# Key pages of a paged attention cache: 64 page copies by SyncE against 16 row gathers by GpSimd

## The chip, the cores and the metric

The kernel runs on one core of one Trainium2 chip. The metric is the device time of one execution in microseconds. Engines go by the names of the profile: PE is TensorE, DVE is VectorE, ACT is ScalarE, POOL is GpSimd and SP is SyncE; SPq and ACTq rows are the DMA issues of SP and ACT.

## The reference, cut to what matters

One inference step of one decoder layer: 256 prompt tokens and 8 decoding sequences of 4 new tokens, D_MODEL 1024. The layer has a gated DeltaNet head group, a stick-breaking attention head group and a mixture of 32 experts (top 4). The change touches the attention of the decoding sequences over their cached past. Each of the 8 sequences has 1024 past keys and values in 8 pages of 128 rows, and a page table says which of 80 pages of the pool hold them.

```python
k_past = cache_k[0, page_table]            # (8 sequences, 8 pages, 128 rows, 8 heads, 64)
z = q . k / sqrt(64) + b_h                 # scores of 4 query tokens, 8 heads, over 1024 keys
beta = sigmoid(z)
A[t, s] = beta[t, s] * prod_{s < j < t} (1 - beta[t, j])
o = A @ v_past
```

The product runs over the keys in their order, so a sequence's scores have to stand in order of position when they are scanned. A row of the cache (8 heads of 64 float32) is 2 KB, a page is 256 KB, a sequence's keys are 2 MB and so are its values.

## The kernel before, in words

The program has a mixer part (projections, attention of the decoding sequences, causal convolution; the first 193 us), a second part (prompt attention and DeltaNet, to about 320 us), and the experts. All three live in blocks in which each engine has its own program, tied by counting semaphores.

**The ring.** All large loads of the mixer go into a ring of 12 slots of 1 MB, used as 6 pairs of 2 MB. `PAIRS` lists what is loaded in order: `w` q, `w` k, K0, K1, `w` v, K2, K3, V0, V1, `w` c0, K4, K5, V2, `w` c1, V3, K6, `w` c2, K7, V4, V5, `w` z, V6, V7 and the two halves of w_out (K and V are the keys and values of a sequence, `w` the input projection's columns for one group). Pair q may be loaded only when pair q-6 has been used (`used`): a weight group when its last projection tile is done (`s_pj`), keys when their scores are done (`s_sc`), values when they are summed (`s_av`). SP issues all of it from one queue in exactly that order (`load_pair`), with small loads after K0, the store of the new keys after K5 and of the new values after V3.

**Keys.** K of a sequence is 8 DMAs of 256 KB, each from a page whose number SP reads into a register (`value_load` from `pt`). Page pg goes to the 32 partitions 32*(pg//2) and up, and of each page the row q*32+r lands in partition r at column block q. So one DMA writes 32 partitions in runs of 2 KB. DVE then turns the tile in place in 32x32 blocks (`turn_keys`, L812, two instructions of 128x2048 a sequence), which puts 32 dimensions on the partitions and 32 rows along the columns. V of a sequence is 8 DMAs of 256 KB over all 128 partitions, in runs of 2 KB.

**PE's order.** PE goes through 29 projection tiles (`tiles`: q 0 to 3, k 4 to 7, v 8 to 11, ba 12, convolution 13 to 24, z 25 to 28), each 8 products over 288 tokens (L509, 16 matmul records a tile). The attention is put between the tiles by hand: `scores(b)` for two sequences after tiles 6, 11, 16, 22 (`SC`, L443), `turn_A(b)` after 10, 15, 19, 25, `values(b)` after 14, 19, 24, 26 (`AV`), `own_heads(b)` after 16, 21, 26, 27, and `spread_new` (L429) after tile 9, which needs the weights of the new tokens (`weights_new`, DVE L835 to L842).

**DVE's order.** DVE turns K0 and K1 before the tiles, K2 after tile 5, K3 after 8, K4 after 12, K5 after 14, K6 after 19, K7 after 20, and does the convolution (`conv`), the scans and the copies in the same queue. The new tokens' work (`mask_new`, `weights_new`) and `scan(0)` stand after tile 7, behind the turning of K2.

**POOL** builds masks and constants (L685 to L763), clears the query blocks (L725), waits at L745 for the small loads, and from tile 13 on multiplies the convolution's outcome with its sigmoid (`silu`, L766 to L772) and squares it (L782). `conv(j)` and the sigmoid of j wait for `silu(j-2)`.

**The start.** ACT issues three DMAs (norm weight, the convolution's state, its taps) and then normalises x; DVE makes the rows (L792, L793), PE turns the taps and the rows (L370, L379) and starts tile 0.

## Time and profile before

| | |
|---|---|
| time of three runs | 1267.64, 1264.80, 1265.74 us, median 1265.74 |
| span of the profiled execution, first to last instruction | 1263.3 us (no other time of it is recorded; 2.4 us under the median) |
| granted TensorE clock, mean | 0.990 of full |
| PE busy over the span | 1208.9 us (96%) |
| DVE, ACT, POOL busy | 445.0, 228.8, 87.5 us |
| bytes moved | 464.23 MB, 367 GB/s over the span |
| mixer part | 0 to 193.7 us |

The profile is one execution. Busy times are read as shares of an engine's time; PE's busy time includes matmuls that run at half clock. A wait names the engine or DMA that came last. The timeline rows give the start and length of consecutive instructions of one line, with the idle time before them in brackets.

### The profile page before, as it was taken

To read this page: it belongs to the slowest core of one execution; us is meant where nothing else is said; L and a number is where in the kernel's file an instruction comes from. 1 tells how busy PE (TensorE), PEld (TensorE's weight loads), DVE (VectorE), ACT (ScalarE), POOL (GpSimd) and SP (SyncE) were. 2 spreads that over 40 slices of the span, in tenths; PEclk is the share of its full clock that TensorE was granted. 3 is DMA by queue.
4 is the path that set the end of the run, shared out by engine and by line. 5 is a ranking of instruction groups with operands and counts; after the bars stand their busy time and mean duration, and the time that the engine had idled before them with its cause. 6 is when DMAs were issued, how large, how long until landed. Compare 5 with 4: busy or idle time off the path is not lost.

```text
span 1263.3 us, 18661 instructions
## 1 busy us (share of the span) xinstructions
PE 1208.9 (96%) x7350; PEld 526.1 (42%) x7350; DVE 445.0 (35%) x922; ACT 228.8 (18%) x389; POOL 87.5 (7%) x163
## 2 busy tenths in 40 slices
PE   8999998999999999999999999999999999999996
PEld 6766566794333333333332333333333333333332
DVE  2567716636422313323222323132231322231324
ACT  2312137325210201101010101010110101020202
POOL 6103303422000000000000000000000000000000
PEclk9999999999999999999999999999999999999999
DMA  9999981209999999999999999999999999999994
GB/s 255 252 314 333 330 307 35 91 7 361 329 369 426 429 428 427 427 427 430 428 427 427 429 428 426 429 427 426 430 429 428 427 428 427 430 425 428 428 426 164
DMA packets 73639, 464.23 MB, mean 367 GB/s; under 512 B 19294, under 2 KB 19294, under 8 KB 46710
## 3 DMA queue, kind: packets, MB, share of 16 engines
q1 hardware_dynamic: 73544, 463.37, 92.0%
q8 instruction: 34, 0.56, 0.2%
q10 hardware_dynamic: 46, 0.18, 0.1%
q14 instruction: 15, 0.12, 0.0%
HBM read 459.82 MB, written 3.70 MB: 367 GB/s over the span
## 4 chain that ended last, share of the span: by engine, by line
PE 60%; DMA 21%; ACT 1%; DVE 1%; issue 1%; SPq 0%; DVEq 0%; ACTq 0%
PE bank L2197 22%; DMA ring<-in_w_up 11%; DMA hoT<-in_w_up 11%; PE bank L2212 9%; PE bank L2235 7%; PE bank L2166 5%; PE bank L2145 4%; PE bank L1494 2%; PE bank L2149 1%; PE bank L2170 1%; PE bank L1285 1%; PE bank L1346 1%; PE bank L1356 1%; PE bank L2262 1%; PE bank L1359 1%
## 5 line engine op out<-in xcount | busy, mean ns | idle before, releaser
L2197 PE MATMUL bank<-ring,work 128*64 128x512 f32 x1280 | 286.2, 601 | 11.4 <-DMA ring<-in_w_up 11.4
L2235 PE MATMUL bank<-ring,work 128*64 128x512 f32 x768 | 171.9, 596 | 6.5 <-ACT work L2329 6.5
L2197 PEld LDWEIGHTS bank<-ring,work 128*64 128x64 f32 x1280 | 91.5, 138 | 204.3 <-issue 198.6
L2385 DVE TENSOR_TENSOR Xw<-Xw,bank 128x512 f32<-128x512 f32 x64 | 44.0, 688 | 225.7 <-PE bank L2166 225.7
L509 PE MATMUL bank<-hoT,ring 128*128 128x288 f32 x448 | 117.6, 419 | 1.7 <-DMA ring<-in_w_in 1.2
L2319 ACT ACTIVATE work<-bank 128x1024 f32<-128x1024 f32 x16 | 16.4, 1024 | 499.5 <-PE bank L2149 471.8
L509 PEld LDWEIGHTS bank<-hoT,ring 128*128 128x128 f32 x448 | 86.0, 196 | 28.8 <-issue 3.6
L2235 PEld LDWEIGHTS bank<-ring,work 128*64 128x64 f32 x768 | 54.2, 137 | 102.4 <-issue 102.4
L2440 DVE COPY work<-bank 128x512 f32<-128x512 f32 x16 | 11.1, 692 | 191.3 <-PE bank L2235 191.3
L2197 PE MATMUL bank<-work 128*64 128x512 f32 x128 | 58.1, 608 | 8.5 <-DMA hoT<-in_w_up 8.5
L2426 DVE TENSOR_SCALAR work<-bank 128x512 f32<-128x512 f32 x32 | 22.0, 689 | 119.8 <-PE bank L2212 118.9
L2166 PE MATMUL bank<-work 128*128 128x512 f32 x128 | 59.2, 605 | 0.0
L2197 PE MATMUL bank<-hoT,work 128*64 128x512 f32 x128 | 58.2, 609 | 0.0
L2212 PE MATMUL bank<-ring,work 128*64 128x512 f32 x256 | 56.7, 595 | 0.0
L2212 PE MATMUL bank<-work 128*64 128x512 f32 x128 | 56.6, 596 | 0.0
L2212 PE MATMUL bank<-hoT,work 128*64 128x512 f32 x128 | 56.6, 595 | 0.0
L2235 PE MATMUL bank<-work 128*64 128x512 f32 x128 | 56.2, 592 | 0.0
L2235 PE MATMUL bank<-hoT,work 128*64 128x512 f32 x128 | 56.2, 592 | 0.0
L2145 PE MATMUL bank<-gq,work 128*128 128x512 f32 x120 | 54.0, 592 | 0.0
L812 DVE STREAM_TRANSPOSE ring<-ring 128x2048 f32<-128x2048 f32 x16 | 36.0, 2288 | 34.1 <-DMA ring<-in_cache_k 34.1
L2431 DVE TENSOR_TENSOR work<-work 128x512 f32<-128x512 f32 x32 | 38.5, 1203 | 18.7 <-ACT work L2325 16.5
L2417 DVE COPY work<-bank 128x384 f32<-128x384 f32 x16 | 8.9, 558 | 97.9 <-PE bank L2262 97.9
(413 smaller groups left out, 1305.3 us busy)
## 6 DMA issues: line engine op xcount, KB each, us to landing
ring<-in_w_up SPq DMA_DIRECT2D x96, 2048.0 KB, 23.2
ring<-in_w_down SPq DMA_DIRECT2D x46, 2048.0 KB, 26.8
work<-in_w_up SPq DMA_DIRECT2D x16, 2048.0 KB, 22.0
hoT<-in_w_up SPq DMA_DIRECT2D x16, 2048.0 KB, 26.5
ring<-in_cache_k SPq DMA_DIRECT2D x64, 256.0 KB, 10.3
ring<-in_cache_v SPq DMA_DIRECT2D x64, 256.0 KB, 9.7
work<-in_w_down SPq DMA_DIRECT2D x16, 1024.0 KB, 24.5
hoT<-in_w_down SPq DMA_DIRECT2D x16, 1024.0 KB, 26.4
```

What stands on the lines that cost most here:

```text
L509: ins = pe.matmul(bank[0:m, i % 2, 0:T], w[:, k, :], hT[:, k, :], start=k == 0, stop=k == KD - 1)
L812: ins = dve.transpose(out=v, in_=v)
L1494: ins = pe.matmul(bank[q, WO_BANK[t, m], :], oT[:, k, toks(t)], w[:, k, :], start=k >= HP if t == 2 else k == (HP if (t, m) == (1, 1) else 0),
L2145: pe.matmul(bank[:, 6 + m, :], Pm[:, t * P:(t + 1) * P], h2[:, t, 512 * m:512 * (m + 1)], start=t == 0, stop=False)
L2166: pe.matmul(bank[:, 4 + n, :], PGT[:, t * P:(t + 1) * P], oo[:, 512 * m:512 * (m + 1)], start=True, stop=True).then_inc(M["y"], 1)
L2197: ins = pe.matmul(bank[CAP * e:CAP * e + CAP, g, :], xT[:, k, CAP * e:CAP * e + CAP], weight(odd, ch + e, k % 2 * RSLOT + 512 * g), start= ...
L2212: ins = pe.matmul(bank[CAP * e:CAP * e + CAP, g, :], xT[:, k, CAP * e:CAP * e + CAP], weight(odd, 6 + e, k % 2 * RSLOT + 512 * g), start=F ...
L2235: ins = pe.matmul(bank[CAP * e:CAP * e + CAP, 4 + m, :], aT[:, k, CAP * e:CAP * e + CAP], weight(odd, ch + e, k % 4 * D + 512 * m), start= ...
L2319: act.activation(xs, bank[:, 6:8, :].rearrange("p b n -> p (b n)"), ACT.Copy).then_inc(M["x_copied"], 1)
L2385: dve.tensor_tensor(x, x, bank[:, 4 + n, :], ALU.add).then_inc(M["y_added"], 1)
L2426: dve.tensor_scalar(gb, hu[:, :, 0], 7.0, None, ALU.min).then_inc(M["gate_clamped"], 1)
L2431: dve.tensor_tensor(ab[:, 512 * half:512 * (half + 1)].rearrange("p (k q) -> p k q", k=4), by_k(ub), by_k(sg), ALU.mult).then_inc(M["act"], 1)
```

## The change

The keys leave SP's queue. For each sequence POOL issues two indirect DMAs (`gather_keys`), each over all 128 partitions, in which partition p fetches 8 KB, that is four consecutive rows of a page. The row indices are worked out once: ACT loads the page table broadcast to the partitions by four DMAs, POOL makes the partition's number within its group of 32 (`krow`, four iotas and a copy), and DVE multiplies and adds (`kidx`). K0 to K2 are gathered after the clearing of the query blocks, K3 after the constants, K4 and K5 ahead of `silu(0)`, K6 and K7 after `silu(3)`. POOL waits after each gather for the instruction's own semaphore, and it waits for K0 to K2 to have landed before it goes on from L744. SP's queue skips the K pairs, and waits for all five page-table loads (80 instead of 16) before pair 2.

A partition now holds rows 4r to 4r+3 of a page instead of rows r, 32+r, 64+r and 96+r. After DVE's turning, the columns of one block belong to positions four apart. The score product therefore writes its columns into PSUM with a step of four elements (16 bytes), so that the scan finds the keys in order.

Several semaphores are merged (`s_ax`, `s_ex`, `s_cs` into others) and `s_ringfree`, which nothing waited for, goes.

```diff
@@ helpers
+        kidx, krow = sb("kidx", [P, 2 * NSEQ], I32), sb("krow", [P, 2])
+        s_keys = [sem(f"keys_loaded{i}") for i in range(4)]
+        cache_k_rows = cache_k[0].rearrange("n (r q) h d -> (n r) (q h d)", q=4)
         def pair_wait(eng, what, n):
+            if what == "K":
+                return eng.wait_ge(s_keys[n % 4], 32 * (n // 4 + 1))
@@ sync
-                    elif what == "K":
-                        for pg in KEY_PAGES:
-                            kb, odd, page = pg // 2, pg % 2, pages[n][pg]
-                            sp.dma_start(tile[32 * kb:32 * kb + 32, 4 * GW * odd:4 * GW * (odd + 1)].rearrange("p (q c) -> p q c", q=4),
-                                         cache_k[0, bass.ds(page, 1)].rearrange("o (q r) h d -> (o r) q (h d)", q=4)).then_inc(done, 16)
-                sp.wait_ge(s_pt, 16)
+                sp.wait_ge(s_pt, 80)
                 for q in range(2, len(PAIRS)):
-                    load_pair(q)
+                    if PAIRS[q][0] != "K":
+                        load_pair(q)
@@ tensor, scores(b)
-                        keys = pair_tile("K", s).rearrange("p (g c) -> p g c", g=8)
+                        keys = pair_tile("K", s).rearrange("p (o q c) -> p o q c", o=2, q=4)
...
                                 ins = pe.matmul(bank[32 * j:32 * j + 32, 6, 256 * (s % 2):256 * (s % 2) + 256]
-                                                .rearrange("p (g r) -> p g r", g=8), Q32[:, s, cb, :], keys[:, :, 32 * cb:32 * cb + 32],
-                                                start=m == 0, stop=m == 3)
+                                                .rearrange("p (o r q) -> p o q r", o=2, q=4), Q32[:, s, cb, :],
+                                                keys[:, :, :, 32 * cb:32 * cb + 32], start=m == 0, stop=m == 3)
@@ scalar, first
                 act.dma_start(wb[0:1, :], norm_mix[0:1, :]).then_inc(s_wb, 16)
+                for kb in range(4):
+                    act.dma_start(kidx[32 * kb:32 * kb + 32, :].rearrange("p (s o) -> p s o", o=2),
+                                  page_table[:, 2 * kb:2 * kb + 2].partition_broadcast(32)).then_inc(s_pt, 16)
                 act.dma_start(crow[0:24], state_conv[0].rearrange("s w c -> (s w) c")).then_inc(s_small, 16)
@@ gpsimd
+                pool.wait_ge(s_id, 1)
+                for kb in range(4):
+                    c(pool.iota(krow[32 * kb:32 * kb + 32, 1:2].bitcast(I32), pattern=[[0, 1]], base=0, channel_multiplier=1))
+                c(pool.tensor_copy(krow[:, 0:1], krow[:, 1:2].bitcast(I32)))
+                pool.sem_inc(s_id, 1)
+                def gather_keys(s):
+                    q = pair("K", s)
+                    if q >= NPR:
+                        used(pool, q - NPR)
+                    for odd in range(2):
+                        pool.indirect_dma_start(out=pair_tile("K", s)[:, 4 * GW * odd:4 * GW * (odd + 1)], out_offset=None, in_=cache_k_rows,
+                                                in_offset=bass.IndirectOffsetOnAxis(ap=kidx[:, 2 * s + odd:2 * s + odd + 1], axis=0),
+                                                engine_sem=s_pool).then_inc(s_keys[s % 4], 16)
+                        c.n += 1
+                        pool.wait_ge(s_pool, c.n)
...
                 pool.memset(Xw[:], 0.0).then_inc(s_q32, 1)
+                pool.wait_ge(s_id, 3)
+                for s in range(3):
+                    gather_keys(s)
...
+                for s in range(3):
+                    pair_wait(pool, "K", s)
                 c(pool.tensor_copy(MASKS[hi, :], MASKS[lo, :]))
...
                 c(pool.memset(nS65[:, HD:HD + 1], -BIG))
+                gather_keys(3)
...
+                gather_keys(4)
+                gather_keys(5)
                 for j in range(12):
+                    if j == 4:
+                        gather_keys(6)
+                        gather_keys(7)
                     silu(j)
@@ vector, first
+                dve.wait_ge(s_pt, 80)
+                dve.wait_ge(s_id, 2)
+                dve.tensor_scalar(kidx[:], kidx[:], 32.0, krow[:, 0:1], ALU.mult, ALU.add).then_inc(s_id, 1)
                 dve.wait_ge(s_t, 1)
```

## Rows read from the trace of the kernel before

**Rows 1.** The page's slices of the span (1/40 each): PE busy, clock, GB/s.

```profile
PE   8999998999999999999999999999999999999996
PEclk9999999999999999999999999999999999999999
GB/s 255 252 314 333 330 307 35 91 7 361 329 369 426 429 428 427 427 427 430 428 427 427 429 428 426 429 427 426 430 429 428 427 428 427 430 425 428 428 426 164
```

**Rows 2.** Waits of PE from 0 to 200 us: total, times, longest.

```profile
PE bank L429 <- DVE work L842: 2.2, 1, 2.2
PE bank L443 <- DVE ring L812: 2.1, 1, 2.1
...
PE bank L509 <- DMA ring<-in_w_in: 1.2, 2, 1.0
```

**Rows 3.** Timeline of PE, 14 to 194 us: start, length, line, idle before.

```profile
46.97 3.66 PE L443 MATMUL bank<-ring,Xw 128*32 128x256 f32 x64 [0.33 <-issue]
...
66.52 5.82 PE L509 MATMUL bank<-hoT,ring 128*128 128x288 f32 x16
...
73.39 4.05 PE L509 MATMUL bank<-hoT,ring 128*128 128x288 f32 x16
...
144.54 1.93 PE L443 MATMUL bank<-ring,Xw 128*32 128x256 f32 x32
148.55 3.25 PE L443 MATMUL bank<-ring,Xw 128*32 128x256 f32 x32 [2.07 <-DVE ring L812]
151.73 4.47 PE L509 MATMUL bank<-hoT,ring 128*128 128x288 f32 x16
```

**Rows 4.** Stretches of the mixer: busy us of each engine, clock, DMA share, GB/s.

```profile
18.00:28.00 10.00, 10.00 (x40) 7.68 (x40) 0.00 (x0) 0.82 (x2) 7.61 (x28) 1.00 1.08 230
28.00:32.00 4.00, 4.00 (x18) 3.16 (x17) 1.03 (x1) 0.41 (x1) 0.00 (x0) 1.00 1.12 149
...
54.00:66.00 12.00, 10.02 (x60) 7.49 (x59) 7.72 (x16) 2.24 (x7) 0.00 (x0) 1.00 1.07 231
66.00:78.00 12.00, 11.73 (x56) 8.98 (x60) 10.12 (x24) 1.42 (x3) 0.00 (x0) 0.86 1.06 386
...
150.00:152.00 2.00, 2.00 (x21) 0.77 (x14) 1.93 (x4) 0.62 (x2) 0.93 (x2) 0.50 1.05 386
```

**Rows 5.** Timeline of DVE: the turning of K2 and of K7.

```profile
57.12 4.51 DVE L812 STREAM_TRANSPOSE ring<-ring 128x2048 f32<-128x2048 f32 x2 [9.21 <-DMA ring<-in_cache_k]
...
143.99 4.50 DVE L812 STREAM_TRANSPOSE ring<-ring 128x2048 f32<-128x2048 f32 x2 [3.54 <-DMA ring<-in_cache_k]
```

**Rows 6.** Timeline of POOL: the clearing, first and fifth silu.

```profile
13.14 3.52 POOL L725 MEMSET Xw<- 128x4096 f32 x1 [3.38 <-issue]
...
100.02 0.81 POOL L769 TENSOR_TENSOR gq<-work 128x256 f32<-128x256 f32 x1 [61.36 <-ACT work L600]
...
124.41 0.88 POOL L769 TENSOR_TENSOR gq<-work 128x256 f32<-128x256 f32 x1 [4.26 <-ACT work L600]
```

**Rows 7.** Timeline of ACT's queue, PE and DVE at the start.

```profile
1.73 0.32 ACTq L538 DMA_DIRECT2D work<-in_conv_w  x1
...
6.64 1.48 PE L370 MATMUL bank<-ident,work 28*128 28x28 f32 x12 [0.53 <-DMA work<-in_conv_w]
9.58 1.97 PE L379 MATMUL bank<-ident,work 128*128 128x128 f32 x8 [1.46 <-DVE work L793]
...
8.05 0.16 DVE L792 RECIPROCAL stat<-stat 128x1 f32<-128x1 f32 x1 [8.05 <-ACT stat L546]
```

**Rows 8.** Timeline of SP's queue: c2 weights, K7.

```profile
119.43 0.67 SPq L306 DMA_DIRECT2D ring<-in_w_in  x1
124.66 4.79 SPq L313 DMA_DIRECT2D ring<-in_cache_k  x8
```

**Rows 9.** The page's costliest groups: DVE reading PSUM at every second column, and densely.

```profile
L2440 DVE COPY work<-bank 128x512 f32<-128x512 f32 x16 | 11.1, 692 | 191.3 <-PE bank L2235 191.3
...
L2426 DVE TENSOR_SCALAR work<-bank 128x512 f32<-128x512 f32 x32 | 22.0, 689 | 119.8 <-PE bank L2212 118.9
```

**Rows 10.** Stretches behind the mixer, same columns as rows 4.

```profile
240.00:260.00 20.00, 20.00 (x684) 19.95 (x681) 8.90 (x14) 5.28 (x10) 17.42 (x12) 1.00 0.02 5
...
400.00:600.00 200.00, 198.48 (x919) 68.92 (x919) 59.93 (x120) 24.25 (x30) 0.00 (x0) 1.00 1.01 428
```

More of the change, by code:

```diff
@@ L182, in slot_count @@
         def slot_count(u):
-            return sum(16 * (NPG if PAIRS[q][0] in "KV" else 1) for q in range(u // 2 % NPR, u // 2 + 1, NPR))
+            return sum(16 * {"K": 0, "V": NPG}.get(PAIRS[q][0], 1) for q in range(u // 2 % NPR, u // 2 + 1, NPR))
         def slot_wait(eng, u):
@@ L195, in build, with used @@
         act_n, dve_n, pool_n = [0], [0], [0]
+        kidx, krow = sb("kidx", [P, 2 * NSEQ], I32), sb("krow", [P, 2])
+        s_keys = [sem(f"keys_loaded{i}") for i in range(4)]
+        cache_k_rows = cache_k[0].rearrange("n (r q) h d -> (n r) (q h d)", q=4)
+        def used(eng, q):
+            what, n = PAIRS[q]
+            if what == "w":
+                eng.wait_ge(s_pj, group_end(n) + 1)
+            elif what == "K":
+                eng.wait_ge(s_sc, n + 1)
+            else:
+                eng.wait_ge(s_av, n + 1)
         s_nsq, s_nstd, s_nrow, s_ntp, s_nev = (
@@ L285, in _ @@
             def _(sp):
-                def used(q):
-                    what, n = PAIRS[q]
-                    if what == "w":
-                        sp.wait_ge(s_pj, group_end(n) + 1)
-                    elif what == "K":
-                        sp.wait_ge(s_sc, n + 1)
-                    else:
-                        sp.wait_ge(s_av, n + 1)
-                pages = {}
                 def load_pair(q):
                     what, n = PAIRS[q]
-                    if what == "K":
-                        pages[n] = [sp.value_load(pt[0:1, NPG * n + pg:NPG * n + pg + 1], min_val=0, max_val=POOL - 1) for pg in range(NPG)]
+                    if what == "V":
+                        pages = [sp.value_load(pt[0:1, NPG * n + pg:NPG * n + pg + 1], min_val=0, max_val=POOL - 1) for pg in range(NPG)]
                     if q >= NPR:
-                        used(q - NPR)
+                        used(sp, q - NPR)
                     tile, done = slot(2 * q, 2), slot_sem(2 * q)
@@ L309, in load_pair @@
                         sp.dma_start(tile.rearrange("p (k n) -> p k n", k=KD), w_out_v[:, :, n * 512:(n + 1) * 512]).then_inc(done, 16)
-                    elif what == "K":
-                        for pg in KEY_PAGES:
-                            kb, odd, page = pg // 2, pg % 2, pages[n][pg]
-                            sp.dma_start(tile[32 * kb:32 * kb + 32, 4 * GW * odd:4 * GW * (odd + 1)].rearrange("p (q c) -> p q c", q=4),
-                                         cache_k[0, bass.ds(page, 1)].rearrange("o (q r) h d -> (o r) q (h d)", q=4)).then_inc(done, 16)
                     else:
-                        for pg, page in enumerate(pages.pop(n)):
+                        for pg, page in enumerate(pages):
                             sp.dma_start(tile[:, GW * pg:GW * (pg + 1)],
@@ L353, in _ @@
                 sp.wait_ge(s_cue, 3)
[L354 removed]
+                sp.dma_start(conv_prompt[0, 0], cst[0:3, :]).then_inc(s_vout, 16)
                 for s in range(NSEQ):
[L356 removed]
+                    sp.dma_start(conv_sample[0, s], cst[3 + 7 * s + 4:3 + 7 * s + 7, :]).then_inc(s_vout, 16)
                 sp.wait_ge(s_kout, 32)
[L358 to L359 removed]
+                sp.wait_ge(s_vout, 32 + 16 * 9)
             @block.tensor
@@ L606, in gate_inputs @@
                         act.activation(ea[r], alog[r, a:NH:2], ACT.Exp)
-                    act.wait_ge(s_ax, 1)
+                    act.wait_ge(s_taps, 3)
                     c(act.activation(ax, ax, ACT.Exp))
-                    act.activation(ax, ax, ACT.Ln, bias=ones[:, 0:1]).then_inc(s_ex, 1)
+                    act.activation(ax, ax, ACT.Ln, bias=ones[:, 0:1]).then_inc(s_q32, 1)
                 def log_squares(k):
@@ L1561, in _ @@
                 pe.wait_ge(s_wo, PARTS + 6)
-                pe.sem_inc(s_ringfree, U_END - U_WO)
                 turn_row(1, 0)
```

22 lines of the change are left out of this document (7 added, 15 removed).

## The prediction

> **What bounds the kernel now.** I read the page's slices first. PE is busy nearly throughout, and after the first quarter the bytes come at a steady 427 to 430 GB/s [rows 1]. The time thus has two parts. In the experts the load stream is full (428 GB/s at a DMA share of 1.01), and it can only begin once the parts ahead have released its buffers: between 240 and 260 us almost nothing is loaded [rows 10]. What the mixer (0 to 193 us) gains or loses moves the start of that stream, so I carry it to the end one for one.
>
> In the mixer I next looked at who makes PE wait. Both PE and the DMA engines look full there: the DMA share is 1.05 to 1.08 in every stretch [rows 4]. The waits tell them apart: after PE's first tile starts at about 15 us its waits come to 2.2, 2.1 and 1.2 us [rows 2] and 0.33 us at the first scores [rows 3]. PE is the bound; the DMA engines are full without being late, except in these places. So a faster key load can give back only those waits and what follows from them.
>
> What follows is seen in the clock. Behind the two long waits the granted clock is low: 0.86 over 66 to 78 us and 0.50 over 150 to 152 us, that is the lower of the two levels, 1.2 GHz [rows 4]. A projection tile there took 5.82 us against 4.05 us elsewhere, and the second half of the last scores 3.25 us against 1.93 us for the first [rows 3]. PE had been idle for 2.2 and 2.07 us just before each drop.
>
> Both long waits lead back to keys. DVE sat 9.21 us until K2 had landed at 57.12 us, and the new tokens' work, for which L429 waits, stands behind that turning in DVE's queue. K7 landed at 143.99 us after 3.54 us of waiting by DVE, and the last scores waited for its turning [rows 5, 2]. Why they land late: with keys in the queue the rate is 230 and 231 GB/s, with values and weights 386 [rows 4], all at a full DMA share.
>
> **The change, part by part.**
>
> *Rate of the keys.* The gather writes 128 partitions in 8 KB runs. I take the 386 GB/s of the values (also 128 partitions), bounds 230 (as now) and 428 [rows 4, 10]. A sequence's 2.1 MB then takes 5.4 us and not 9.1, eight sequences 44 and not 73: 29 us of DMA time are set free, none of it on the path by itself.
>
> *The wait at L429.* K0 to K2 are gathered when POOL has cleared the query blocks, at 13.14 + 3.52 = 16.7 us [rows 6]. With the v weights that is 8.4 MB, 22 us at 386 GB/s: all landed by about 40 us, and K2 is wanted by DVE at 57.12 - 9.21 = 47.9 us [rows 5]. DVE then ends this turning 9 us earlier and is ready for the new tokens when PE delivers their scores. I count the wait and its clock as gone: 2.25 + (5.82 - 4.05) = 4.0 us. The 0.33 us before the first scores goes too.
>
> *The waits for weights.* The two waits for w_in, 1.2 us together, come because c1 and c2 queue behind keys: c2 was issued at 119.43 us, with K6 just ahead [rows 8]. Now SP passes the keys by. Gone: 1.2 us.
>
> *The wait for K7.* SP issued it at 124.66 us [rows 8]. POOL now issues K6 and K7 after the fourth silu, about 120 us on the old clock, 117 with what is gained till then. 4.2 MB at 386 GB/s are 11 us, so K7 lands at about 131. DVE wants it at about 134 and PE can bear some 3 us more. Gone: 2.07 + (1.93 + 3.25 - 3.66) + (4.47 - 4.15, what the tiles after such a block otherwise take) = 3.9 us.
>
> Together 4.0 + 0.3 + 1.2 + 3.9 = 9.4 us.
>
> *The start.* Four more DMAs stand in ACT's queue ahead of the convolution's state and taps. At 0.32 to 0.52 us an issue that is 1.3 to 2.1 us; the taps landed at 6.64 us, PE needs 1.48 us for them and is wanted at 9.58 [rows 7], so 1.46 us are slack and at most 0.6 us fall on the path. DVE's first instruction now waits for all page tables; its next one was due at 8.05 us [rows 7]. Issued by 3.4 us and landing 2.5 to 5 us later (the page table took under 3 us, the taps 4.9), they come at 5.9 to 8.4: 0 to 0.5 us. They are 1,024 pieces of 8 bytes that mix with the loads of x. The nearest row is 28 to 32 us, in which some 1,500 small pieces held the rate at 149 GB/s where the neighbours had 230, which is 1.4 us of loading lost [rows 4]; two thirds of that are 1.0 us, in full on the path at worst. Bounds 0 and 2.1 us; I take 1.2.
>
> *The gathers on POOL.* No row shows one. Bounds for one instruction with its wait: 0.32 us, an issue by ACT, and 3.52 us, POOL's longest instruction [rows 7, 6]. I take about 1.1, between them. The first six delay the masks behind them by 7 us; `pair_wait` holds POOL until about 40 us, the masks are then done by 43 and DVE asks for them at about 60. K3 is issued at about 50 and wanted after 70. K4 and K5 lie in POOL's 61 us of idle time [rows 6]. Only K6 and K7 stand where POOL has work: it had 4.26 us to spare before the fifth silu [rows 6]. Four gathers at 1.1 us take just that. Behind the fifth silu are the seventh convolution, the turning of K6, the eighth convolution and the turning of K7, about 16 us of DVE, and PE wants the last by about 142. Counted back, a gather may take 2.0 us before anything is late. Cost taken: 0. Iotas and copy lie in POOL's 3.38 us wait before the clearing.
>
> *The PSUM step.* The scores write with a step of 16 bytes. The trace has no matmul with a stepped output. The nearest row is DVE reading PSUM at every second column: 689 ns for 512 elements, dense 692 [rows 9], so no cost. The other bound is half rate, as those same matmuls show at the low clock: four blocks of 3.66 us would take 14.6 us more. A matmul's column also takes long as it is: 4.05 us for 16 times 288 columns, 0.88 ns a column [rows 3]. I take 0, by the nearest row.
>
> The Trainium skill speaks against this part: "PSUM — Partial Sum Buffer", Specifications, lists "Cachelines: 8-byte (any non-contiguous AP slows matmuls significantly)". It gives no price; no run here has shown it, and the DVE row, which keeps within that 8-byte grain, can't refute it. By the rule the sum would end above the present time if the scores took more than about 1.56 times as long.
>
> *The rest.* The 64 issues that leave SP (0.6 us each in [rows 8]) and the merged semaphores cost or give nothing: SP isn't waited for, except in the order counted above.
>
> The sum is 9.4 - 1.2 = 8.2 us: a span of 1255.1 for 1263.3. The median of the runs is 2.4 us above the profiled span, and I keep that distance: 1257.5 us.
>
> **The rivals.**
>
> *A, stepped writes are slow.* Place: the four score blocks, in line on PE. Price 14.6 us at half rate: 1257.5 + 14.6 = 1272.1. It decides from 1.56 times the present duration (8.2 / 14.6). For it: 16 bytes is wider than any step in the trace. Against: rows 9 and the slow pace of a column. 0.15.
>
> *B, slow gathers.* At 3.5 us each, K6 and K7 hold the fifth silu until about 131 us. DVE's 16 us then end at about 148, 6 us after PE wants them, and with the low clock behind it the third stall costs 7.8 us instead of none: 1257.5 + 7.8 = 1265.3, no change. For it: POOL's gathers there coincide with a DVE that is busy for most of the time. 0.15.
> The Trainium skill, "SBUF — State Buffer", the box on the SWDGE trap, has a mechanism for it: GpSimd can't write descriptors while DVE runs a two-port copy, and a DMA of 620 ns took 3100. No run here shows it.
>
> *C, one stall stays.* K7 or the new tokens' work is still late, for instance since the gathers come at 230 GB/s as now or share the engines with V4 and V5: 3.9 of the 9.4 are not got, 1261.4. 0.15.
>
> *D, no effect.* The mixer gains, but the full load stream swallows it, or the start costs all its bounds and more: 1264 to 1266. The empty stretch 240 to 260 us [rows 10] speaks against it. 0.05.
>
> **How the numbers follow.** Forecast (gain of 5 to 12 us) 0.50, A 0.15, B 0.15, C 0.15, D 0.05. A run of this kernel can tell about 0.2%, 2.5 us, from no change. Faster by more: forecast and C, 0.64 after a little off for its edge. Within: B and D, less B's slow tail, 0.16. Slower: A and B's tail, 0.20. Range: 1254.0, the 9.4 with a start at no cost and 2 us more where DMA time set free helps elsewhere, to 1270.0, which takes in B, C, D and a partly priced A. The likeliest case's own range is 1254 to 1261.
>
> **What would show it.** Right: no wait of L429 and L443, no clock under 1.00 at 60 to 80 and 140 to 160 us, score blocks at 3.7 us, the mixer's end at 185 to 186 us, DMA rate above 350 with keys in flight, PE's first tile at 15 to 17 us. Wrong: score blocks at 5 us or more (A), gathers on POOL of over 2 us and DVE waiting for a silu (B), DVE waiting for `in_cache_k` after 120 us (C), the mixer shorter but the end unmoved (D).

## The result

The changed kernel took 1269.63 us (median of 20 runs, 1265.94 to 1275.26), the kernel before 1265.22 us (20 runs, 1261.34 to 1268.05). The ratio is 1.003, with a 95% interval of 1.0019 to 1.0041: slower by about 0.3%. The forecast was 1257.5 us and faster. The time lies in the range of 1254.0 to 1270.0, but that is no merit of the forecast: the upper end was there for slow stepped writes and slow gathers, and neither happened.

The waits of PE over the first 200 us of the changed kernel (total, times, longest) answer to [rows 2]. Neither L423, the old L429, nor the scores at L437 wait for anything, and nothing waits for `in_w_in`. One new line is longer than all that went:

```profile
PE bank L364 <- DMA work<-in_conv_w: 12.8, 1, 12.8
PE bank L360 <- DMA Xw<-in_norm_mix: 2.4, 1, 2.4
```

The timeline of PE in the changed kernel shows the new wait, tile 0 behind it, the first and the last score blocks and the last tile:

```profile
18.91 1.48 PE L364 MATMUL bank<-ident,work 28*128 28x28 f32 x12 [12.79 <-DMA work<-in_conv_w]
20.32 4.66 PE L373 MATMUL bank<-ident,work 128*128 128x128 f32 x24
25.45 17.90 PE L503 MATMUL bank<-hoT,ring 128*128 128x288 f32 x64 [0.47 <-ACT hoT L548]
...
56.94 3.66 PE L437 MATMUL bank<-ring,Xw 128*32 128x256 f32 x64
...
149.29 3.66 PE L437 MATMUL bank<-ring,Xw 128*32 128x256 f32 x64
152.88 4.15 PE L503 MATMUL bank<-hoT,ring 128*128 128x288 f32 x16
...
188.77 4.04 PE L503 MATMUL bank<-hoT,ring 128*128 128x288 f32 x16
```

Tile 0 starts at 25.45 us, where it had started at 15.15: 10.3 us late. (The x64 in its row are the first four tiles.) The last tile starts at 188.77 us where it had started at 187.94. So 9.5 us of the 10.3 came back inside the mixer. The scores, now written with the step of 16 bytes, take 3.66 us a block to the digit, also where half of a block had run at the low clock [rows 3].

ACT's queue and DVE's first instruction in the changed kernel (timeline; an ACTq row is the issue, not the landing) against [rows 7]:

```profile
1.37 3.09 ACTq L532 DMA_DIRECT2D kidx<-in_page_table  x4
4.49 0.52 ACTq L534 DMA_DIRECT2D work<-in_state_conv  x1
5.04 3.21 ACTq L535 DMA_DIRECT2D work<-in_conv_w  x1
```
```profile
17.56 0.23 DVE L815 TENSOR_SCALAR kidx<-kidx,krow 128x16 int32<-128x16 int32 x1 [17.56 <-DMA kidx<-in_page_table]
```

The four tables were issued by 4.5 us and landed at 17.5 us, and the taps, next but one in the same queue, at 18.9. DVE and PE each waited for one of the two. On the page the queue of ACT has 1,134 packets for 0.18 MB where it had 46:

```profile
q0 software_dynamic: 2304, 16.78, 3.3%
...
q10 hardware_dynamic: 1134, 0.18, 0.1%
```

The extra 1,088 are 1,024 pieces of 8 bytes and 64 completion writes. By the trace's DMA records a piece itself takes 7 ns, but they run from 3.7 to 16.6 us, with no pause over 0.12 us between two of them. If each of the 16 DMA engines gets 64, that is one per 0.20 us. Packets of x and of the weights (4 KB at 169 ns, 2 KB at 99 ns on average) run between them, and are slowed as well. From 8 to 11 us the two queues (q1 is SP's, q10 ACT's) moved only this:

```profile
q1 hardware_dynamic: 59, 0.14, 13.1%
q10 hardware_dynamic: 336, 0.00, 5.2%
```

In the kernel before SP's queue moved 709 packets from 6 to 11 us. The last packet of x began at 10.4 us (8.1 in the kernel before), the first of the weights at 11.2 (6.4). Tile 0 did not wait for these here, because the taps were later still.

The keys themselves behave as hoped for. Stretches of the changed kernel (columns as in [rows 4]): with gathers in flight the rate is 419 GB/s, then DMA idles, and the clock is full where it had been 0.86:

```profile
30.00:46.00 16.00, 16.00 (x66) 12.02 (x65) 6.05 (x3) 1.64 (x4) 10.12 (x34) 1.00 1.03 419
46.00:60.00 14.00, 14.00 (x107) 10.26 (x109) 7.23 (x11) 7.30 (x20) 8.00 (x26) 1.00 0.19 61
60.00:78.00 18.00, 18.00 (x104) 13.76 (x97) 9.91 (x31) 3.51 (x9) 0.00 (x0) 1.00 0.76 258
```

The gathers on POOL (timeline of the changed kernel, one of the first six, then the four around the fifth silu):

```profile
27.22 0.94 POOL L705 DMA_INDIRECT ring<-in_cache_k,kidx  x1 [0.30 <-DMA ring<-in_cache_k,kidx]
...
126.24 0.98 POOL L705 DMA_INDIRECT ring<-in_cache_k,kidx  x1 [0.15 <-issue]
127.53 1.08 POOL L705 DMA_INDIRECT ring<-in_cache_k,kidx  x1 [0.30 <-DMA ring<-in_cache_k,kidx]
128.91 1.15 POOL L705 DMA_INDIRECT ring<-in_cache_k,kidx  x1 [0.31 <-DMA ring<-in_cache_k,kidx]
130.37 1.23 POOL L705 DMA_INDIRECT ring<-in_cache_k,kidx  x1 [0.30 <-ACT work L597]
131.68 0.86 POOL L790 TENSOR_TENSOR gq<-work 128x256 f32<-128x256 f32 x1
```

With the 0.3 us behind each these are 1.2 to 1.5 us a gather, under the 2.0 us from which something would have been late. The silu behind them cost DVE 1.1 us, and PE nothing.

The profiled executions differ by 4.6 us (1267.9 and 1263.3 us), the mixers only by 0.8. The rest stands further behind: the first expert's first matmul starts at 329.90 us for 327.16, 1.9 us more of difference, and the experts take 938.0 us for 936.1. The experiments come to both.

### The profile page after: what moved, and what is told of

The parts are those of the page before. It is cut to its first block, busy times and chain, and to the rows that moved or that the text cites. A ratio compares the mean times of both kernels' runs of the same rounds, so it can differ in the third digit from the quotient of the medians.

```text
span 1267.9 us, 18576 instructions
## 1 busy us (share of the span) xinstructions
PE 1208.1 (95%) x7350; PEld 524.0 (41%) x7350; DVE 445.1 (35%) x923; ACT 228.4 (18%) x389; POOL 103.5 (8%) x184
## 3 DMA queue, kind: packets, MB, share of 16 engines
q10 hardware_dynamic: 1134, 0.18, 0.1%
## 4 chain that ended last, share of the span: by engine, by line
PE 60%; DMA 21%; ACT 1%; DVE 1%; issue 1%; SPq 0%; DVEq 0%; ACTq 0%
PE bank L2225 22%; DMA ring<-in_w_up 11%; DMA hoT<-in_w_up 10%; PE bank L2240 9%; PE bank L2263 7%; PE bank L2194 5%; PE bank L2173 4%; PE bank L1523 2%; PE bank L2177 1%; PE bank L2198 1%; PE bank L1314 1%; PE bank L1375 1%; PE bank L2290 1%; PE bank L1385 1%; PE bank L1388 1%
## 5 line engine op out<-in xcount | busy, mean ns | idle before, releaser
L503 PE MATMUL bank<-hoT,ring 128*128 128x288 f32 x448 | 115.6, 414 | 0.5 <-ACT hoT L548 0.5
L503 PEld LDWEIGHTS bank<-hoT,ring 128*128 128x128 f32 x448 | 84.8, 193 | 26.2 <-issue 2.9
L2357 ACT ACTIVATE work<-bank 128x512 f32<-128x512 f32 x32 | 19.1, 597 | 128.1 <-PE bank L2271 128.1
## 6 DMA issues: line engine op xcount, KB each, us to landing
work<-in_w_down SPq DMA_DIRECT2D x16, 1024.0 KB, 24.5
```

The source lines that it names most:

```text
L503: ins = pe.matmul(bank[0:m, i % 2, 0:T], w[:, k, :], hT[:, k, :], start=k == 0, stop=k == KD - 1)
L2357: act.activation(aT[:, 4 * half:4 * half + 4, :].rearrange("p k s -> p (k s)"), bank[:, half, :], ACT.Copy)\
```

## The experiments

All twelve ran beside runs of the kernel before on the same chip. "Tile 0" and "last tile" are the starts of PE's first and last projection tile.

**1 to 4: where the start is lost.** The first moves the four loads behind the taps, and DVE's instruction behind the rows:

```diff
                 act.dma_start(wb[0:1, :], norm_mix[0:1, :]).then_inc(s_wb, 16)
-                for kb in range(4):
-                    act.dma_start(kidx[32 * kb:32 * kb + 32, :]...
...
                 act.dma_start(crow[0:24], ...)
                 act.dma_start(crow[24:NROW], conv_w[0]).then_inc(s_small, 16)
+                for kb in range(4):
+                    act.dma_start(kidx[32 * kb:32 * kb + 32, :]...
...
@@ vector
-                dve.wait_ge(s_pt, 80); dve.wait_ge(s_id, 2); dve.tensor_scalar(kidx[:], ...)
...
                 dve.tensor_copy(convw, by_j[:, :, 24:NROW]).then_inc(s_taps, 1)
+                dve.wait_ge(s_pt, 80); dve.wait_ge(s_id, 2); dve.tensor_scalar(kidx[:], ...)
```

> The changed kernel with the four page-table loads moved behind the taps in ACT's queue, and DVE's index instruction moved behind the row normalisation. Theory (the 1,024 pieces of 8 bytes hold up whatever follows them on ACT's queue, and DVE's wait for them holds up the rows): tile 0 starts at 15 to 18 us instead of 25.4, PE no longer waits 12.8 us for the taps, and the mixer ends at about 184.5 to 187 us; median 8 to 10 us under the changed kernel's, so 4 to 6 us under the kernel before. Rival (the small pieces delay the loads of x and of the weights as well, wherever they stand): tile 0 still starts after 20 us, and less than half of the 10 us comes back.

Measured: 1268.48 us against 1265.57 (ratio 1.0016, 0.9997 to 1.0034). Waits of PE from 14 to 190 us:

```profile
PE bank L503 <- DMA ring<-in_w_in: 6.0, 1, 6.0
PE bank L408 <- issue: 3.4, 1, 3.4
PE bank L447 <- DVE hoT L905: 0.2, 1, 0.2
```

The taps came at 6.5 us, as the theory said, but tile 0 started at 20.04 us: now it waited for the first weights. SP, which waits for the tables before its small loads, issued these at 18.39 us (15.93 in the kernel before). They then ran beside the gathers, and PE stood at L408 (the masks, which need them) for 3.4 us. The rival is right in its place: the small pieces hold up whatever has to land in their time, on either queue. In its size it is not, since 5.4 of the 10.3 us came back, more than half. The clock was low for 6.8 us over the start of tile 0 and again from 41 us, and the median was 2.9 us above the kernel before, though the interval still reaches 1, and not 4 to 6 us under it.

How the small loads were held up can be read from the queues from 28 to 36 us, where q0 is POOL's (the gathers, 8 KB a packet) and q1 SP's (390 and 343 of them are such packets and pieces of 32 bytes):

```profile
q0 software_dynamic: 437, 3.20, 97.5%
q1 hardware_dynamic: 437, 0.03, 3.8%
```

One packet of SP's queue went for each of POOL's. The 384 pieces of 32 bytes took from 25.5 to 37.1 us; in the changed kernel, where they ran without gathers, 1.9 us.

The second puts the four loads on SP's queue, behind the k weights, with DVE's instruction as in the first.

```diff
                 load_pair(1)
+                for kb in range(4):
+                    sp.dma_start(kidx[32 * kb:32 * kb + 32, :].rearrange("p (s o) -> p s o", o=2),
+                                  page_table[:, 2 * kb:2 * kb + 2].partition_broadcast(32)).then_inc(s_pt, 16)
                 sp.wait_ge(s_pt, 80)
```

> The changed kernel with the four page-table loads on SP's queue behind the k weights, DVE's index instruction behind the row normalisation. Theory: ACT's queue is as in the kernel before, tile 0 starts at 15.2 us; the tables land after the k weights at about 20 us, the first gather starts at 20 to 24 us, the first scores wait for nothing; mixer's end at 184 to 185 us, median 4 to 6 us under the kernel before. Rival (gathers that start later than 20 us bring the old stall at the first scores back): a wait of 1 us or more at the first scores.

Measured: 1267.75 us against 1265.57 (1.0023, 1.0006 to 1.0041). Tile 0 at 14.73 us and no wait at the first scores, as the theory said; but SP's small loads went out only at 25.80 us, PE waited 4.1 us for them at the masks, and the clock was low for 6.8 us there. Last tile at 185.48 us, but the median was above the kernel before and not 4 to 6 us under it. The start was mended and the tables' lateness showed in the next place.

The tables landed later than the 20 us expected, though nothing ran beside them. From 20 to 25 us these pieces (532 of the packets) were all that the DMA engines had, but for one instruction fetch:

```profile
q1 hardware_dynamic: 567, 0.00, 5.0%
```

If 16 engines share them, that is still one per 0.15 us, with the engines busy for 5% of the time. In the kernel before 1,358 packets, most of them small, ran in the 2 us from 28 to 30. So the pieces of this load are slow by themselves, and another queue only adds to it. Why they are slow alone stays open; no run varied their size or what they read apart from their number.

The third changes the shape and leaves the places: one load of the whole table to every partition, 128 pieces of 256 bytes, into columns that were kept free for the table anyway.

```diff
-                for kb in range(4):
-                    act.dma_start(kidx[32 * kb:32 * kb + 32, :].rearrange("p (s o) -> p s o", o=2),
-                                  page_table[:, 2 * kb:2 * kb + 2].partition_broadcast(32)).then_inc(s_pt, 16)
+                act.dma_start(ptall, page_table.rearrange("s n -> (s n)").partition_broadcast(P)).then_inc(s_pt, 16)
@@ sync
-                sp.dma_start(pt, page_table.rearrange("(o s) n -> o (s n)", o=1)).then_inc(s_pt, 16)
-                sp.wait_ge(s_pt, 80)
+                sp.wait_ge(s_pt, 16)
@@ vector
-                dve.wait_ge(s_pt, 80)
+                dve.wait_ge(s_pt, 16)
...
-                dve.tensor_scalar(kidx[:], kidx[:], 32.0, krow[:, 0:1], ALU.mult, ALU.add).then_inc(s_id, 1)
+                for kb in range(4):
+                    r = slice(32 * kb, 32 * kb + 32)
+                    ins = dve.tensor_scalar(kidx[r].rearrange("p (s o) -> p s o", o=2),
+                                            ptall[r].rearrange("p (s n) -> p s n", n=NPG)[:, :, 2 * kb:2 * kb + 2],
+                                            32.0, krow[r, 0:1], ALU.mult, ALU.add)
+                ins.then_inc(s_id, 1)
```

> The changed kernel with one load of the whole table to all partitions (128 pieces of 256 bytes) in ACT's queue where the four loads stood, SP's own small load gone, DVE's index work in four instructions at the same place at the head of its queue. Theory (the number of pieces is what costs, each waiting its turn behind a packet of SP's queue): 8 pieces an engine instead of 64, so the table lands by 5 to 7 us, the taps at 7 to 9 us, tile 0 starts at 15 to 16.5 us, and the median is 3 to 6 us under the kernel before although DVE still waits first thing. Rival (it is the place at the head of ACT's and DVE's queues, whatever is loaded): tile 0 after 20 us.

Measured: 1262.33 us against 1265.57 (0.9984, 0.9968 to 1.0). PE's timeline in this run: the taps at 9.89 us, a little late by the theory, tile 0 at 15.97.

```profile
9.89 1.48 PE L364 MATMUL bank<-ident,work 28*128 28x28 f32 x12 [3.82 <-DMA work<-in_conv_w]
11.30 3.89 PE L373 MATMUL bank<-ident,work 128*128 128x128 f32 x24
15.97 15.79 PE L503 MATMUL bank<-hoT,ring 128*128 128x288 f32 x64 [0.78 <-ACT hoT L546]
```

Same places, an eighth of the pieces, and 9.5 of the 10.3 us are back. The place at the head of the queues is not what costs. The last tile started at 177.44 us, 10.5 us before that of [rows 3]'s profile, yet the median gained only 3.2 us, and the interval of the ratio reaches 1. That is taken up in 7 and 8 and in the table behind 11.

The fourth is the kernel before with the four loads alone, read by nothing.

```diff
                 act.dma_start(wb[0:1, :], norm_mix[0:1, :]).then_inc(s_wb, 16)
+                for kb in range(4):
+                    act.dma_start(kidx[32 * kb:32 * kb + 32, :].rearrange("p (s o) -> p s o", o=2),
+                                  page_table[:, 2 * kb:2 * kb + 2].partition_broadcast(32)).then_inc(s_kt2, 16)
```

> The kernel before, with the same four page-table loads ahead of the convolution's state in ACT's queue; nothing reads them, and only SP waits for them at the end of the mixer. Theory (the pieces hold up the taps on ACT's queue): PE waits for the taps until about 16 to 19 us, tile 0 starts at 22 to 26 us, and since the old stalls stay, the median is 7 to 11 us above the kernel before. Rival (only DVE's wait at the head of its queue costs, the taps would have come in time): tile 0 at 15 to 17 us and the median within 2 us of the kernel before.

Measured: 1270.13 us against 1265.57 (1.0044, 1.0028 to 1.006).

```profile
19.68 1.48 PE L372 MATMUL bank<-ident,work 28*128 28x28 f32 x12 [13.46 <-DMA work<-in_conv_w]
21.09 4.23 PE L381 MATMUL bank<-ident,work 128*128 128x128 f32 x24
26.09 15.79 PE L511 MATMUL bank<-hoT,ring 128*128 128x288 f32 x64 [0.78 <-ACT hoT L556]
```

The loads alone give the whole late start; DVE's wait isn't needed for it. But the cost was 4.6 us and not the 7 to 11 I had expected. Of the stalls of [rows 2] only one was left, of 2.2 us at the last scores, without a low-clock stretch behind it, and 0.2 us for `in_w_in`: a PE that starts 11 us late lets the loads run ahead. Its last tile started at 190.13 us, only 2.2 us later than in the kernel before. In this kernel a late start is partly paid for by stalls that it makes needless.

**5: the number of pieces.** Two of the four loads on the kernel before:

```diff
-                for kb in range(4):
+                for kb in range(2):
                     act.dma_start(kidx[32 * kb:32 * kb + 32, :]...
```

> The kernel before with two of the four table loads ahead of the convolution's state on ACT's queue (512 pieces of 8 bytes), used by nothing. Theory (each piece takes a turn of its own beside SP's packets, about 0.24 us for each of the 32 pieces of a DMA engine): PE's taps come at 11 to 13.5 us (6.6 with none, 19.6 with four), tile 0 at 18.5 to 21 us. Rival (a fixed delay from any such load): taps at 17 us or later, as with four.

```profile
12.92 1.48 PE L372 MATMUL bank<-ident,work 28*128 28x28 f32 x12 [6.82 <-DMA work<-in_conv_w]
```

Measured: 1269.28 us against 1265.99 (1.0017, 1.0001 to 1.0034), tile 0 at 19.47. The taps come at 6.64, 12.92 and 19.68 us with 0, 512 and 1,024 pieces: 6.3 and 6.8 us for each 512, so 0.20 to 0.21 us for each of the 32 that a DMA engine gets. The rival is out: the delay grows with what is loaded. These two runs alone can't tell pieces from loads, as each load has 256 pieces, and the wide load, 8 pieces an engine in one load, put off the taps by 3.3 us in experiment 3: 3.3, 6.3 and 13.0 us for one, two and four loads would fit as well. The DMA records speak for the pieces: they run without a pause (at most 0.14 us between two starts) from the first load into the next, so the time is spent between pieces and not between loads. But a piece has no single price: 0.4 us for each of the wide load's, 0.20 to 0.21 here, 0.15 alone.

**6: the layout alone.** The kernel before with runs of 8 KB over 32 partitions, and with the stepped scores (the two lines of the change, not shown again):

```diff
-                            sp.dma_start(tile[32 * kb:32 * kb + 32, 4 * GW * odd:4 * GW * (odd + 1)].rearrange("p (q c) -> p q c", q=4),
-                                         cache_k[0, bass.ds(page, 1)].rearrange("o (q r) h d -> (o r) q (h d)", q=4)).then_inc(done, 16)
+                            sp.dma_start(tile[32 * kb:32 * kb + 32, 4 * GW * odd:4 * GW * (odd + 1)],
+                                         cache_k[0, bass.ds(page, 1)].rearrange("o (r q) h d -> (o r) (q h d)", q=4)).then_inc(done, 16)
...
```

> The kernel before with the layout alone: SP still copies each page in a DMA of its own to 32 partitions, but in runs of 8 KB (partition r takes rows 4r to 4r+3), and the scores are written with the step of 16 bytes. Theory (what made keys slow is that a DMA writes 32 partitions only, and the step costs nothing): DMA rate with keys in flight stays at 230 to 250 GB/s, the stalls at L429 and at the last scores stay at about 2 us each, a score block takes 3.66 us, and the median is within 2 us of the kernel before. Rival (the 2 KB runs made it slow): above 300 GB/s with keys in flight, both stalls gone, mixer 7 to 9 us shorter.

Measured: 1262.80 us against 1265.80 (0.9976, 0.9963 to 0.9989). The stretches show the rate with keys in flight, in this kernel and, in the second fence, with gathers (experiment 8):

```profile
46.00:50.00 4.00, 4.00 (x68) 2.18 (x66) 0.61 (x2) 1.69 (x2) 0.00 (x0) 1.00 1.02 258
50.00:54.00 4.00, 4.00 (x20) 3.10 (x17) 0.00 (x0) 1.27 (x2) 0.00 (x0) 1.00 1.02 260
```
```profile
30.00:34.00 4.00, 4.00 (x17) 2.64 (x16) 3.49 (x2) 0.41 (x1) 3.08 (x15) 1.00 1.02 414
34.00:38.00 4.00, 4.00 (x18) 3.16 (x17) 2.01 (x2) 0.45 (x2) 0.93 (x5) 1.00 1.01 410
```

A run four times as long brings 246 (the kernel before again, 46 to 54 us) to 258 GB/s; 128 partitions bring 414. So it is not the length of the runs that held the keys back; the 32 partitions are what is left of the theory, though a gather differs also in its queue. Values, which SP copies to 128 partitions in 2 KB runs, came at 386 [rows 4]. Where the theory erred: with these few per cent L429 no longer waited, and the last scores waited 1.7 us, with the clock up after that:

```profile
139.20 1.93 PE L443 MATMUL bank<-ring,Xw 128*32 128x256 f32 x32
142.82 1.93 PE L443 MATMUL bank<-ring,Xw 128*32 128x256 f32 x32 [1.68 <-DVE ring L812]
```

The last tile started at 180.57 us, 4.5 us before that of the second profile of the kernel before (7, below) with the same start of tile 0, though a low-clock stretch fell at 33 us. So half of the mixer's gain is to be had without any gather, and the median is clearly under the kernel before, by 3.0 us where I had expected at most 2. The stepped scores take 1.93 us for 32 here, as the dense ones do, so the step in PSUM costs nothing that shows.

**7 and 8: the same kernels again.** The kernel before, and the wide load of experiment 3, with no edit.

> The kernel before, unchanged, for a second profile of it and as a measure of what the same program scatters by. Expected: ratio 1 within its interval; tile 0 at 15.2 us and the last tile of the mixer at 187.9 us within 0.5 us of the first profile; the part behind the mixer may differ by 1.7 us for each low-clock piece of 3.4 us. If instead the mixer itself scatters by several us, the milestones of single profiles can't carry the comparison.

> The wide load at the head of the queues, the same kernel as the third run, for a second profile. If the 3.9 us by which its second part was longer come from where its low-clock stretches happened to lie, this profile may show 0 to 4 us there; if they come with the shorter mixer, it shows 3 to 4 us again. Last tile of the mixer at 177.4 us within 0.5.

Measured: the kernel before 1265.42 against 1265.80 us (0.9999, 0.9981 to 1.0016); the wide load 1257.56 against 1265.80 (0.9943, 0.9923 to 0.9962). The wide load's last tile was at 177.94 us, where 177.44 had been expected; the middle was 2.5 us and the experts 1.4 us shorter than in the first profile of it. The kernel before had its last tile at 185.07 us and not at 187.94: my expectation of 0.5 us was wrong. Its first four tiles took 15.79 us where [rows 3]'s profile had 17.82, and only one of its two stalls was followed by a low-clock stretch. So one profile of the kernel before is good to some 3 us, and the first was on the slow side.

**9: both mends together.** The wide load behind the taps, DVE's work behind the rows; run twice.

```diff
                 act.dma_start(crow[24:NROW], conv_w[0]).then_inc(s_small, 16)
+                act.dma_start(ptall, page_table.rearrange("s n -> (s n)").partition_broadcast(P)).then_inc(s_pt, 16)
@@ vector
                 dve.tensor_copy(convw, by_j[:, :, 24:NROW]).then_inc(s_taps, 1)
+                dve.wait_ge(s_pt, 16)
+                dve.wait_ge(s_id, 2)
...
```

> The one wide load of the table placed behind the taps in ACT's queue, and DVE's four index instructions behind the row normalisation: everything the start needs comes first. Theory: taps at 6.6 us as in the kernel before, tile 0 at 15.2 to 15.5 us, last tile of the mixer 0.5 to 1 us earlier than with the wide load ahead of the taps (177.4), so 176.5 to 177. If the mixer's gain went to the end one for one the median would be 11 us under the kernel before; the first run with the wide load gave only 3 to 5 of 10.5 us, so the theory that low-clock stretches behind the mixer take the rest back expects 3 to 7 us under it, with more than one 3.4 us low-clock piece between the mixer's end and the first expert.

> The wide load behind the taps once more, beside the version above on the same chip. Last tile of the mixer at 177 to 181 us (180.2 in the first profile, whose first four tiles took 18.8 us; 15.8 is possible and would give 177); the median 4 to 8 us under the kernel before.

Measured: 1260.21 against 1265.80 us (0.9951, 0.9932 to 0.9971) and 1256.18 against 1265.99 (0.9936, 0.9913 to 0.9958). This is 0.5 to 0.6% faster than the kernel before; from experiment 3's kernel, whose second run had 0.9943, the intervals don't tell it apart. The first profile missed its 176.5 to 177: its last tile was at 180.16 us, and 3.0 us of that lie in its first four tiles. The waits of PE from 14 to 190 us in the second run are all that is left in the mixer (the first line is the boundary between two parts):

```profile
PE bank L1286 <- PEq L295: 1.8, 1, 1.8
PE bank L503 <- ACT hoT L546: 0.8, 1, 0.8
PE bank L447 <- DVE hoT L908: 0.5, 1, 0.5
```

In that run tile 0 started at 14.35 and the last tile at 175.81 us, 9.3 us before the second profile of the kernel before.

**10: the wide load on SP's queue**, in front of x, in the place of SP's small load; the rest as in 9.

```diff
-                act.dma_start(ptall, page_table...
@@ sync, first
+                sp.dma_start(ptall, page_table.rearrange("s n -> (s n)").partition_broadcast(P)).then_inc(s_pt, 16)
                 load_x()
```

> One wide load of the table (128 pieces of 256 bytes) first in SP's queue in place of its small load; ACT's queue as in the kernel before; DVE's index work behind the rows. Theory: the pieces cost SP's queue under 0.5 us as nothing else competes yet, taps at 6.6 us, tile 0 at 14.5 to 16 us, no stall at L411, the mixer's last tile at 175.5 to 178 us; the median 5 to 9 us under the kernel before. Rival (the pieces delay x as well): tile 0 after 17 us.

Measured: 1261.64 against 1265.99 us (0.9971, 0.9949 to 0.9992). Tile 0 started at 16.72 us, later than the theory's 14.5 to 16 and just short of the rival's 17: the packets of x ran from 4.0 to 9.9 us (2.2 to 8.1 in the kernel before), and PE waited 2.2 us for DVE's rows. So the rival's mechanism was there, at a small price. Last tile at 178.18. The intervals of 9 and 10 overlap.

**11: the changed kernel again.**

> The changed kernel, unchanged, for a second profile. Expected: tile 0 at 25.4 us and the mixer's last tile at 188.8 us, each within 0.5 us, since a start that waits for the taps has no room to scatter; the median 3 to 5 us above the kernel before. The two profiles of the kernel before had their last tile at 187.9 and 185.1 us, so the mixer is 0.8 to 3.7 us longer than theirs and the rest of the difference should lie in low-clock pieces.

Measured: 1268.99 against 1265.99 us (1.0023, 1.0005 to 1.004). Tile 0 at 25.37 and the last tile at 188.65 us, as expected.

**What lies behind the mixer.** With fourteen profiles the rest can be read. The mixer is taken to the start of its last tile, the middle from there to the first expert's first matmul. The low-clock stretches come in pieces of 3.4 us.

| profile | last tile | middle | low clock in it | experts | low clock in the last 70 us before the tail |
|---|---|---|---|---|---|
| before | 187.94 | 139.2 | 3.4 | 936.1 | no |
| before again | 185.07 | 140.9 | 6.8 | 935.9 | no |
| changed | 188.77 | 141.1 | 6.8 | 938.0 | yes |
| changed again | 188.65 | 140.6 | 6.8 | 938.1 | yes |
| 1 | 189.88 | 140.6 | 6.8 | 937.9 | yes |
| 2 | 185.48 | 139.8 | 6.8 | 936.4 | no |
| 3 | 177.44 | 143.1 | 10.2 | 938.0 | yes |
| 3 again | 177.94 | 140.5 | 6.8 | 936.6 | no |
| 4 | 190.13 | 138.9 | 3.4 | 936.1 | no |
| 5 | 187.24 | 142.3 | 10.2 | 937.9 | yes |
| 6 | 180.57 | 142.6 | 10.2 | 937.9 | yes |
| 9 | 180.16 | 140.2 | 6.8 | 938.1 | yes |
| 9 again | 175.81 | 141.7 | 6.8 | 936.3 | no |
| 10 | 178.18 | 140.8 | 6.8 | 936.2 | no |

A piece costs the middle about 1.7 us, as 3.4 us at half the clock should. In the experts the load stream is the bound: counted from the DMA records it takes 724.4 to 724.6 us from its 150th to its 460th MB in all fourteen profiles. All seven profiles with a low-clock piece near the end took 937.9 us or more, all seven without it 936.6 or less. My reading is that an early piece is lost in PE's waits for loads and a late one isn't; no run moved a piece on purpose.

**The first four tiles.** They took 15.8 us in seven of the profiles and 17.3 to 18.8 in the others, both profiles of the changed kernel among these. In experiment 1, where the granted clock over the start of tile 0 is recorded, it was 0.50 (stretches with the work of L503 alone: PE, weight loads, clock, DMA share, GB/s):

```profile
20.00:24.00 4.00, 3.96 (x9) 2.87 (x10) 0.50 1.08 409
24.00:38.00 14.00, 13.74 (x57) 10.45 (x55) 1.00 1.02 408
```

In the other six the trace's record of the clock only begins 3.2 to 6.1 us behind the start of tile 0 (the view fills the gap with 1.00), and until then a matmul takes twice as long, as here in the changed kernel:

```profile
25.45:29.70 4.25, 4.25 (x9) 3.07 (x10) 1.00 1.07 275
29.80:43.20 13.40, 13.40 (x56) 10.26 (x54) 1.00 1.03 418
```

In the seven quick ones the record, at full clock, begins before tile 0. In all fourteen the four tiles take 15.8 us plus half of the time from tile 0 to the full clock, within 0.1 us. So this is the low clock again, 2.1 us in both profiles of the changed kernel and 2.0 in the first of the kernel before. What decides when it rises stays open: experiment 4's PE began its work at 19.68 us after 13.5 us of waiting, the changed kernel's at 18.91 after 12.8, and the first had the full clock from 24.5 us, the second from 29.8.

## Why the prediction was wrong, point by point

**The gain in the mixer was right, in place and about in size.** It was put at 9.4 us. In experiment 9's second run, which has the keys' change and hardly a cost at the start, the last tile came 9.3 us before that of the kernel before on the second profile, and the medians of its two runs were 5.6 and 9.8 us under the kernel before, around the 8.2 forecast. In the changed kernel 9.5 of 10.3 lost us came back. That the sizes agree to 0.1 us is luck: single profiles scatter by 3 us. Nor is all of it the gathers' own: by experiment 4 a late start by itself undoes most of the stalls, and by experiment 6 the layout alone gives about half. All three stalls went: L429, the two waits for `in_w_in`, and K7. With gathers in flight the rate was 410 to 419 GB/s and I had taken 386.

**The clock behind the stalls was priced as certain and isn't.** I counted 1.8 us of it at L429 and the same at the last scores, since there the clock fell behind waits of 2.2 and 2.07 us. In the other profiles a wait of 2.6 us at the last scores had a low-clock stretch behind it and waits of 2.2 (experiment 4) and 2.0 us (experiment 5) in the same place had none, nor had 1.7 us at L429. The first profile had both.

**The step that failed is the start**, costed at 1.2 us with bounds of 0 and 2.1. It measured 10.3. I priced 1,024 pieces of 8 bytes from the stretch of 28 to 32 us [rows 4], in which some 1,500 small pieces cost 1.4 us of loading. That row says what small pieces take from the rate of the others, and I carried its pace over to these. What counts is when the last of them is through, and when what stands behind them in that queue gets its turn: the 1,024 took 12.9 us beside SP's packets. Experiments 3 and 5 show that the delay goes with the number and shape of the pieces, experiment 4 that nothing else of the change is needed. Two things make it: these pieces came at one per 0.15 us an engine with nothing beside them (experiment 2), and a second queue adds its own packets in between (experiment 1). The pace alone is unexplained. The issue time, on which I spent the first half of the step, was also longer than the 0.32 to 0.52 us of [rows 7]: 3.09 us for four, then 3.21 us for the taps alone.

The Trainium skill has the rule that I should have set beside it: "DMA: Bandwidth & Descriptors", Queues, rings and completion order, says that a DMA engine goes round the queues it has work for, a packet from each, where a packet is typically 9 to 17 descriptors. The runs agree that the queues take turns, but a turn here was a single piece: 437 packets of POOL's queue and 437 of SP's in 8 us of experiment 1.

**That the mixer's change goes to the end one for one** holds within some 6 us, not closer: from the last tile's start to the end the fourteen profiles took 1075.0 to 1081.1 us. The changed kernel's profile ended 4.6 us later than the one before with a mixer only 0.8 longer: 1.9 us came in the middle and 1.9 in the experts, each with one low-clock piece more or at a worse place. Between the second profiles of the two the mixer is 3.6 us longer, the middle 0.3 shorter, the experts 2.2 longer. Both pairs have a low-clock piece near the end in the changed kernel and none in the kernel before. Why the pieces fall where they do is open; I saw them move with the same kernel run twice.

**The rivals.** A, slow stepped writes: wrong, 3.66 us as before; the rule of the Trainium skill that speaks against it ("PSUM — Partial Sum Buffer", Specifications) didn't show at this step and with 32-bit elements. B, slow gathers: wrong, 0.93 to 1.23 us each; the longest stood beside a busy DVE (but the very first took 1.18 us, DVE nearly idle), so DVE's work cost a gather at most 0.3 us. C, one stall stays: wrong. D came nearest, with "the start costs all its bounds and more", and had 0.05.

## What to carry to other kernels

A load made of many small pieces is priced by its number of pieces, at a pace read from a trace of just such pieces (0.15 to 0.4 us each here, against under 0.03 for others), and then by everything that stands behind it in its own queue; the bytes say nothing. Beside a second busy queue each piece can wait for one packet of that. Give a broadcast of a small table whole rows (128 pieces of 256 bytes here) and let compute pick, or put it where nothing urgent lands in its time. And before a small stall is removed, see what fed it: a late start had hidden most of the same stalls, so two changes that mend one thing don't add up.

## What the runs showed that I had not expected

- Four loads of 256 pieces of 8 bytes landed 16 us after their issue began, beside running loads, at 7 ns a piece; the taps behind came at 6.64, 12.92 and 19.68 us with 0, 512 and 1,024 pieces ahead.
- With nothing beside them the same pieces ran at 106 a us, the DMA engines 5% busy.
- Beside gathers of 8 KB packets SP's queue moved one small piece for each such packet (437 to 437 in 8 us).
- With gathers of 128 rows of 8 KB in flight all DMA together moved 410 to 419 GB/s, near the 428 of the experts' stream, at 0.94 us of POOL a gather as a rule.
- DMAs to 32 partitions gave 246 GB/s in 2 KB runs and 258 in 8 KB runs.
- A matmul that writes PSUM with a step of 16 bytes ran as fast as a dense one (3.66 us for 64 in both).
- PE's first four tiles took 15.8 us or 17.3 to 18.8, by how long the clock stayed low behind the start of tile 0.
- At the last scores the granted clock fell behind stalls of 2.07 and 2.6 us, and stayed up behind stalls of 1.7, 2.0 and 2.2.
